# A transformer block pair on one Trainium2 core: when a mixer's weight halves are rounded, when shared key parts are copied, and where rests of outputs stand in the vector queue

## What is computed

```python
proj = h @ w_in                      # c_q 256, c_kv 128, k_rope 32, conv_in 3*512, gate_logits 2*1024
q    = rms_norm(c_q)  @ w_uq         # 8 heads x (64 + 32)
kv   = rms_norm(c_kv) @ w_ukv        # 8 heads x (64 + 64)
q_nope, k_nope = rms_norm(...)       # per head
q_rope, k_rope = apply_rope(rms_norm(...))   # k_rope is one key part shared by all 8 heads
o_attn = causal softmax(q k^T / sqrt(96)) v
u      = causal 3-tap convolution of (gate_c * xv);  o_conv = gate_b * u
merged = sum over the two branches of sigmoid(gate) * (o_branch @ w_branch)
y      = merged @ w_out
```

## Time and profile before

| what | value |
|---|---|
| median of 3 runs | 1012.15 us |
| the profiled execution, its own time | 1011.21 us |
| its span, first to last instruction | 1009.4 us |
| TensorE busy | 982.6 us (97%) |
| TensorE weight loads busy | 917.6 us (91%) |
| VectorE busy | 774.3 us (77%) |
| ScalarE busy | 535.0 us (53%) |
| GpSimd busy | 11.8 us (1%) |
| mean granted TensorE clock | 0.995 |

### The profile page before, as it was taken

How to read it: one execution, slowest core, us unless ns; L and a number is a source line. 1 busy time by engine, 2 the same in 40 slices (tenths; PEclk the granted TensorE clock), 3 DMA queues, 4 the chain that set the end, 5 groups by cost and what they waited for, 6 DMA issues and landing times.

```text
span 1009.4 us, 17305 instructions
## 1 busy us (share of the span) xinstructions
PE 982.6 (97%) x7016; PEld 917.6 (91%) x7016; DVE 774.3 (77%) x1420; ACT 535.0 (53%) x927; POOL 11.8 (1%) x32
## 2 busy tenths in 40 slices
PE   5999999999899999999999999999999999999996
PEld 4999998998898999999998988789999988988895
DVE  6999999879976787685776588556778776677665
ACT  5454554437566555353655545664555555455453
POOL 0000000004000000000000000000000000000000
PEclk9999999999999999999999999999999999999998
DMA  9997999865572664678665535364445555545431
GB/s 336 351 344 272 344 343 340 303 212 210 200 253 99 218 213 181 219 239 224 244 227 184 192 126 209 125 183 136 157 173 178 188 188 189 208 168 181 174 106 42
DMA packets 33677, 213.92 MB, mean 212 GB/s; under 512 B 3773, under 2 KB 6717, under 8 KB 8894
## 3 DMA queue, kind: packets, MB, share of 16 engines
q1 hardware_dynamic: 33310, 211.78, 59.5%
q10 hardware_dynamic: 288, 1.05, 0.3%
HBM read 210.19 MB, written 2.62 MB: 211 GB/s over the span
## 4 chain that ended last, share of the span: by engine, by line
PE 80%; DVE 9%; ACT 4%; DMA 4%; issue 2%; SPq 0%; DVEq 0%; ACTq 0%
PE bank L216 78%; DMA sb_raw<-wts 3%; DVE sb_ring L195 2%; ACT sb_ring L192 2%; PE bank L219 2%; ACT sb_tmp L192 1%; DVE sb_junk L204 1%; DVE sb_tq L195 1%; DVE sb_tmp L195 1%; DMA R<-rows 1%; DVE sb_tmp L201 1%; ACT R L192 0%; DMA sb_x<-xt 0%; DVE R_512r L195 0%; DVE sb_tmp L198 0%
## 5 line engine op out<-in xcount | busy, mean ns | idle before, releaser
L216 PE MATMUL bank<-sb_h,sb_ring 128*128 128x258 f32 (+2 forms) x3776 | 496.0, 292 | 4.1 <-DVE sb_h L201 3.9
L216 PEld LDWEIGHTS bank<-sb_h,sb_ring 128*128 128x128 f32 x3776 | 475.5, 190 | 17.8 <-issue 5.9
L195 DVE TENSOR_TENSOR sb_ring<-sb_raw,sb_ring 128x1024 fp32r<-128x1024 f32 (+1 forms) x324 | 385.6, 1205 | 10.4 <-ACT sb_ring L192 10.3
L192 ACT ACTIVATE sb_ring<-sb_raw 128x1024 fp32r<-128x1024 f32 (+1 forms) x324 | 320.4, 1037 | 80.3 <-DMA sb_raw<-wts 47.5
L216 PE MATMUL bank<-R_512r,sb_ring 128*128 128x256 f32 (+1 forms) x1608 | 225.7, 301 | 0.0
L216 PEld LDWEIGHTS bank<-R_512r,sb_ring 128*128 128x128 f32 x1608 | 211.4, 188 | 12.0 <-issue 0.5
L216 PE MATMUL bank<-sb_ring,sb_h 128*128 128x512 f32 (+1 forms) x504 | 112.5, 378 | 0.0
L216 PEld LDWEIGHTS bank<-sb_ring,sb_h 128*128 128x128 f32 x504 | 87.4, 188 | 16.6
L204 DVE CUSTOM_DVE_ANT_0 sb_junk<-sb_raw,sb_csil,sb_cols 128x1024 bf16<-128x1024 f32 x72 | 92.3, 1282 | 1.8
L216 PE MATMUL bank<-R_1024r,sb_ring 128*128 128x512 f32 (+1 forms) x576 | 91.6, 320 | 0.0
L216 PEld LDWEIGHTS bank<-R_1024r,sb_ring 128*128 128x128 f32 x576 | 82.0, 188 | 8.2
(11 more groups left out here) (158 smaller groups left out, 555.8 us busy)
## 6 DMA issues: line engine op xcount, KB each, us to landing
sb_raw<-wts SPq DMA_DIRECT2D x193, 1024.0 KB, 4.9
sb_raw<-wts SPq DMA_DIRECT2D x3, 512.0 KB, 3.6
scratch<-R SPq DMA_DIRECT2D x1, 1536.0 KB
sb_x<-xt ACTq DMA_DIRECT2D x2, 512.0 KB, 5.0
R<-scratch SPq DMA_DIRECT2D x2, 508.0 KB, 9.1
sb_raw<-wts SPq DMA_DIRECT2D x1, 768.0 KB, 4.5
sb_raw<-wts SPq DMA_DIRECT2D x1, 640.0 KB, 3.9
R<-scratch SPq DMA_DIRECT2D x2, 258.0 KB, 5.8
```

The source lines that it names most:

```text
L192: return Issued(self.e and self.e.activation(o, i, func, **kw))
L195: return Issued(self.e and self.e.tensor_tensor(*a))
L216: return Issued(self.e and self.e.matmul(o, w, m, start=start, stop=stop, skip_group_check=True))
```

## The change

It has three parts. `self.apart` is set before the two conv_in projections that precede the queries instead of at the attention's start. `heads_kr(t)` moves from `head_keys` into `heads(t)`. In the attention, `o_lo_1` and the `fill` ahead of it move out of `between` into a new stage `rest`, which runs in the next half step, behind that step's `scores_1`, `masked_1` and `exp_1`.

```diff
@@ -872,6 +872,7 @@
         cut = M1_ORDER.index(("qkv", 0))
+        self.apart = True
         run(M1_ORDER[:cut], SUMS_AT)
@@ -917,11 +918,11 @@
             done(ab[0], ("t_q", t))
             done(ab[1], ("t_q", t))
+            self.add("heads_kr", t, ko)
 
         def head_keys():
             for t in range(2):
                 self.add("heads_k", t)
-                self.add("heads_kr", t, ko)
             done(ko, ("heads_kr", 0), ("heads_kr", 1))
@@ -966,15 +967,22 @@
                 if o_b:
                     hp, o = o_b.pop()
                     self.add("o_hi_1", hp, o)
+                    o_rest.append((hp, o))
+
+            def rest(n):
+                if o_rest:
+                    hp, o = o_rest.pop()
                     self.fill()
                     self.add("o_lo_1", hp, o)
                     done(o, ("o_1", hp))
 
-            o_b = []
-            yield from in_half_steps(scores, turn, pv, between)
+            o_b, o_rest = [], []
+            yield from in_half_steps(scores, rest, turn, pv, between)
+            yield
+            rest(11)
 
         def start():
-            self.side, self.every, self.apart = attention(), STEP_1 / 2, True
+            self.side, self.every = attention(), STEP_1 / 2
@@ -1349,12 +1357,14 @@
-def in_half_steps(scores, turn, pv, between):
+def in_half_steps(scores, rest, turn, pv, between):
 
     for n in range(11):
         yield
-        for i, stage in ((0, scores), (2, turn), (3, pv)):
-            if 0 <= n - i < 8:
+        for i, stage in ((0, scores), (None, rest), (2, turn), (3, pv)):
+            if i is None:
+                stage(n)
+            elif 0 <= n - i < 8:
                 stage(n - i)
         yield
         between(n)
```

## The result

| | before | after |
|---|---|---|
| median of 13 runs each, us | 1011.53 | 1014.54 |
| lowest to highest, us | 1010.47 to 1013.13 | 1013.29 to 1016.79 |
| profiled execution, its own time / span, us | 1011.21 / 1009.4 | 1013.35 / 1011.6 |

The ratio is 1.0029, with a 95% interval of 1.0020 to 1.0037: the change makes the kernel 3.0 us slower. The two profiled executions lie 2.1 us apart.

A forecast was written before the change was run, and what follows sets the result against it. It took TensorE's mixer 1 waits, largely the chain VectorE, ScalarE, bank, as the bound (7.3 us at most). Second bank +1.54, clock +1.1, attention -0.75 made +1.9 us: 1012.15 to 1014.0 us, range 1010.2 to 1016.0.

The forecast's parts named there:

- the gap cost another 1.6 us: Before the change, TensorE's work after the 2.96 us wait at 276.48 ran at 0.50 clock, losing 1.6 us.
- Queries, 0.95 us: `c_sums_out` follows one `hi` half instead of two, so TensorE starts the queries 0.95 us earlier, at 234.6.
- VectorE chain 0.27 later behind the queries: VectorE's `lo` waits 1.0 us for conv_in(2)'s second `hi` half and starts at 242.57 instead of 242.30.
- Bank of conv_out(0): At conv_in(3)'s tile 1, TensorE waits 1.7 us for the later-freed bank 4 and goes on at 255.33.
- VectorE 0.6 late at the evacuation of gates(1): Delays through conv_in(3) and conv_out(2) make VectorE's chain 0.6 us late at `gate_in` (ends 0 and 1.0).
- First bank 275.5, second 282.97 after 3.95 us: Turned heads' banks: TensorE passes the first 1.0 us sooner, then idles 3.95 us, passing the second 1.54 us later.
- Clock, 1.1 us: After the second turned bank's gap, the clock, falling 2.0 to 2.9 us into it, costs 1.1 us.
- late fall: Rival: clock falls at the gap's end (1.6 us) or VectorE is 1 us late; +2.4 to +3.5, 1015.0; chance 0.16.
- Attention, 0.75 us: Last attention wait (319.85, 1.39 us): mask first starts `exp_1` 1.8 us sooner, a `hi` half costs 0.95; gain 0.75.
- faster: Rival: second turned bank is free when TensorE comes (no change at release 282.2); -3.1 us, 1009.0; chance 0.12.
- Warm: Rival: same release of the second turned bank, but the clock stays up; +0.8 us, 1012.9; chance 0.17.
- does nothing net: Rival: waits in mixer 1 only change place; within 1 us of before, 1012.1; chance 0.10.

The follow-up runs named there:

- e3: Only `o_lo_1` and its `fill` moved behind the next mask, against the kernel before: 1010.79 us, ratio 0.9995.
- e6: The whole change, with both `conv_gate_shift` copies of a conv_out put ahead of the `hi` halves: 1013.38 us, ratio 1.0028 to the kernel before.
- e1: Only the earlier `self.apart` (halves from the convolution on), against the kernel before: 1014.12 us, ratio 1.0025.
- e5: The whole change, but with gates(3)'s weight unit alone rounded whole again: 1011.45 us, ratio 1.0000 to the kernel before.
- e2: Only `heads_kr` moved into `heads(t)`, against the kernel before: 1011.55 us, ratio 1.0000.
- e4: The whole change without the earlier `self.apart`, its two other moves kept: 1010.88 us, ratio 0.9992 to the kernel before.
- e7: e4 with four banks in turn for the turned heads in place of two: 1008.57 us, ratio 0.9971 to the kernel before.
- e10: e7 with `turn_1` ahead of `scores_1` in each attention half step: 1007.46 us, ratio 0.9960 to the kernel before.

## Why the prediction came out as it did

Its sign was right, its range holds the time (1014.54 in 1010.2 to 1016.0), and its main step is what happened. That its 1014.0 lies within 0.6 us of the time is in part luck: it added 1.9 us to a kernel before of 1012.15 (three runs), and the medians of 13 runs moved by 3.0, from 1011.53. It had given 0.48 to "within 0.2%", and the change of 0.29% lies beyond that, in the 0.40 of "slower". Step by step:

- *The opening reading, "the gap cost another 1.6 us":* **wrong.** TensorE's slow work after the gap did take 1.6 us more, but e3, with the clock up, reaches the second bank no sooner (281.40 against 281.43). Of the 7.3 us called the most that can be won, these 1.6 could not be won by themselves.
- *Queries, 0.95 us:* 1.04 in the trace (0.09 of it the trace's own lead), and no wait left but 0.17.
- *VectorE chain 0.27 later behind the queries:* the `lo` half started at 242.47 instead of 242.30, after a wait of 0.98 us for its `hi`. 0.17; right in mechanism.
- *Bank of conv_out(0):* expected wait 1.7, going on at 255.33; measured 1.34, going on at 255.23. The time of going on was right; the wait was shorter because the 99th matmul ends at 253.89 by the profile.
- *VectorE 0.6 late at the evacuation of gates(1):* 278.56 instead of 278.02, 0.54, or 0.63 with the lead of 0.09. e6 shows that this chain, and not the bank, is what counts.
- *First bank 275.5, second 282.97 after 3.95 us:* measured 275.46, and 282.90 after 3.86. e1 shows that part 1 alone brings it, e5 that it hangs on the one half.
- *Clock, 1.1 us:* **mis-sized.** 1.40 us in the profiled execution, 2.5 in e1's, against 1.1. The step took the fall to come 2.0 to 2.9 us into the gap, so that part of the low clock is spent waiting. The fall came at the gap's end: 0.94 over 280 to 283 puts it at 282.6, as the rival "late fall" has it. That the same kernel meets the low clock at different places from run to run is borne out by the kernel before and e3 (last section).
- *Attention, 0.75 us:* **mis-sized.** -0.42 in the change, and 0.9 us of waits in place of 1.39 in e3. The step put `exp_1` 1.8 us sooner, so the last mask (317.77 before) at about 316.0; in e3 it started at 316.45, after 0.81 us of waiting for the scores, which TensorE finished later because of the 0.56 us wait that the same part adds. The rest of the output no longer delayed the mask, TensorE did.
- *Part 2 costs and gains nothing by itself:* e2, 1.0000.

The sum was +1.9 for the profiled execution, and it measured +2.1 (1011.21 to 1013.35). That these lie so close is partly luck: the two errors of size add up (0.3 and 0.3, both making it slower), so that the attention ends 2.45 us late, and 0.30 us of it is gone further on, for no reason that the prediction had.

The medians moved by 3.0. What the other runs have on top of the profiled one was not traced. That it is the clock is argued, not shown. For it: the changed kernel's profiled run is among its three lowest (1013.29, 1013.35, 1013.64), and e1's, with the clock low for longer, is the second highest of its eight. e6's seven runs lie in two groups: the four from 1012.9 to 1013.4 all have a mean granted clock of 0.996, the three from 1015.3 to 1015.8 all 0.994. As an estimate from these figures, which have three digits only, 0.002 of 1012 us is 2.0 us of TensorE's work, near the 2.3 us between the medians of the groups. Against it as the only cause: in the changed kernel the three runs at 0.994 do lie high (1015.0 to 1015.5), but the highest of all, 1016.79, has 0.995, and 1014.65 has 0.997. And e4's traced execution, 0.8 us above its median with the clock at 1.00 around the turned heads, has 1.18 us of waits for `sb_ring` near 475 and 481, against 0.19 in the kernel before; such waits vary as well.

Of the rivals, "faster" fell with the second bank at 282.90, above its 282.2; "late fall" (clock price 1.6) is nearest to what the median shows. "Warm" fell with the clock at 0.50 over 283 to 286, and "does nothing net" with an interval that starts at 1.0020.

## What to carry to other kernels

When work is deferred on an in-order engine, follow it to where it lands: half a rounding (0.95 us) moved out of one bank's release went into the next bank's, where nothing hid it. Look for a second release right behind the one that is repaired; here it was free only 0.04 us before it was used, in a trace that shows no wait there, and part 2's 0.6 us came to nothing for that reason. Where two buffers are reused on a chain through two other engines, two more free ones (e7, 2.1 us against e4 by the ratios) did more than any reordering tried here (parts 2 and 3 together 0.8, e10 1.1).

## What the runs showed of the hardware

- The same gap need not bring the clock down. Before: 2.96 us idle, and 3.4 us at 0.50 (1.2 GHz). e3, with the same instructions up to there: 2.97 us idle, and the clock stayed at 1.00. In e2 the fall came after a gap of 2.36 us, with TensorE running again: 0.96 over 275 to 277 puts it at 276.8, and TensorE had gone on at 275.69.
- The length of the low clock varies as well. In e1 it was low from inside the gap to nearly 289 (means below):

```profile
280.00:283.00 3.00, 0.00 (x0) 0.00 (x0) 2.08 (x3) 2.97 (x6) 0.00 (x0) 0.81 0.60 251
283.00:286.00 3.00, 2.92 (x14) 2.89 (x15) 2.27 (x4) 1.29 (x3) 0.00 (x0) 0.50 0.67 235
286.00:290.00 4.00, 4.00 (x26) 3.97 (x26) 0.66 (x2) 0.98 (x2) 0.00 (x0) 0.66 0.85 348
```

  Worked out: 1.14 + 3.00 + 2.72 us, together 6.9 us at 0.50, twice the 3.4 us of the kernel before. TensorE's lost time behind the gap in front of the second bank was 1.40 us in the changed kernel's trace and 2.5 in e1's; in the kernel before and in e5 the clock fell ahead of that bank, and cost little or nothing, as the bank came no sooner. One profile gives one draw of this price.
